# One recurrence chunk's values by quarters, output products by kind, bonus steps and one projection tile moved

## The reference

```python
def step(S, inp):
    r_t, w_t, k_t, v_t, kk_t, a_t = inp
    s_kk = jnp.einsum('bhij,bhj->bhi', S, kk_t)
    S = (S * w_t[:, :, None, :]
         - s_kk[..., None] * (a_t * kk_t)[:, :, None, :]
         + v_t[..., None] * k_t[:, :, None, :])
    return S, jnp.einsum('bhij,bhj->bhi', S, r_t)
...
wkv = (wkv7_scan(r4, heads(decay(w0_f, wf_lo, w_up_f)), k_f, v4, kk, heads(a_f), False)
       + wkv7_scan(r4, heads(decay(w0_b, wb_lo, w_up_b)), k_b, v4, kk, heads(a_b), True))
...
bonus = ((jnp.sum(r4 * k_f * rk, axis=-1, keepdims=True)
          + jnp.sum(r4 * k_b * rk, axis=-1, keepdims=True)) * v4).reshape(B, T, RWKV_DIM)
```

## Time and profile before

| | |
|---|---|
| median of 3 timed runs | 1910.21 us |
| lowest, highest | 1906.68, 1910.99 us |
| profiled execution, its own time | 1912.8 us |
| its span, first to last instruction | 1911.0 us |
| mean granted clock of PE | 0.95 of full speed |
| PE busy | 1721.5 us, 90% |
| PE weight loads busy | 1374.7 us, 72% |
| DVE busy | 921.0 us, 48% |
| ACT busy | 304.5 us, 16% |
| POOL busy | 171.5 us, 9% |

### The profile page before, as it was taken

How to read it: one execution, slowest core, us unless ns; L and a number is a source line. 1 busy time by engine, 2 the same in 40 slices (tenths; PEclk the granted TensorE clock), 3 DMA queues, 4 the chain that set the end, 5 groups by cost and what they waited for, 6 DMA issues and landing times.

```text
span 1911.0 us, 30563 instructions
## 1 busy us (share of the span) xinstructions
PE 1721.5 (90%) x12568; PEld 1374.7 (72%) x12568; DVE 921.0 (48%) x1848; ACT 304.5 (16%) x691; POOL 171.5 (9%) x159
## 2 busy tenths in 40 slices
PE   8999999999999999999999999999999765655666
PEld 3888888999888989679999998887787221211213
DVE  5766667897886366644676136852532000000000
ACT  2200000011210002422111114322323000000001
POOL 3000000000133310001000003630001000000000
PEclk9999999999999999999999999998999887888878
DMA  9433443765852214126545863102378999999996
GB/s 376 143 131 129 132 132 125 260 222 179 323 203 92 85 48 152 66 86 224 197 162 179 296 206 129 66 25 89 110 300 354 432 429 435 430 429 435 431 429 292
DMA packets 47336, 428.23 MB, mean 224 GB/s; under 512 B 5395, under 2 KB 6004, under 8 KB 16124
## 3 DMA queue, kind: packets, MB, share of 16 engines
q1 hardware_dynamic: 37584, 389.07, 52.8%
q10 hardware_dynamic: 9644, 37.59, 5.8%
HBM read 425.59 MB, written 1.05 MB: 223 GB/s over the span
## 4 chain that ended last, share of the span: by engine, by line
PE 70%; DMA 18%; DVE 7%; issue 2%; ACT 2%; POOL 0%; POOLq 0%; SPq 0%; ACTq 0%; DVEq 0%
DMA arena<-experts_ring_dram 18%; PE bank L1081 17%; PE bank L1215 14%; PE bank L1265 9%; PE bank L1311 6%; PE bank L1722 3%; PE bank L1411 3%; PE bank L1409 3%; PE bank L1793 2%; PE bank L2104 2%; PE bank L1589 1%; ACT arena L2408 1%; DVE tiny L3336 1%; PE bank L1464 1%; PE bank L1454 1%
## 5 line engine op out<-in xcount | busy, mean ns | idle before, releaser
L1081 PE MATMUL bank<-arena 128*128 128x128 f32 (+1 forms) x2208 | 355.7, 323 | 0.5 <-ACT arena L2629 0.5
L1081 PEld LDWEIGHTS bank<-arena 128*128 128x128 f32 x2208 | 325.5, 192 | 28.4 <-issue 1.8
L2104 PE MATMUL bank<-arena 128*32 128x512 f32 x1400 | 218.5, 780 | 140.2 <-DMA arena<-experts_ring_dram 140.2
L2104 PEld LDWEIGHTS bank<-arena 128*32 128x32 f32 x1400 | 58.8, 138 | 293.2 <-issue 293.1
L1215 PE MATMUL bank<-arena 128*128 128x256 f32 x880 | 193.9, 379 | 0.0
L1215 PEld LDWEIGHTS bank<-arena 128*128 128x128 f32 x880 | 167.1, 190 | 23.1 <-issue 0.5
L1265 PE MATMUL bank<-arena 128*128 128x128 f32 x1456 | 162.9, 275 | 0.0
L1265 PEld LDWEIGHTS bank<-arena 128*128 128x128 f32 x1456 | 162.8, 192 | 0.1
L3745 DVE TENSOR_TENSOR arena<-arena,bank 128x512 f32<-128x512 f32 x8 | 5.5, 688 | 238.2 <-PE bank L2104 238.2
L1311 PE MATMUL bank<-arena 128*128 128x128 f32 x880 | 102.8, 275 | 0.0
L1311 PEld LDWEIGHTS bank<-arena 128*128 128x128 f32 x880 | 100.9, 192 | 0.2
(11 more groups left out here) (533 smaller groups left out, 2480.9 us busy)
## 6 DMA issues: line engine op xcount, KB each, us to landing
arena<-dense_dram SPq DMA_DIRECT2D x169, 1024.0 KB, 4.9
arena<-experts_ring_dram SPq DMA_DIRECT2D x41, 4096.0 KB, 26.9
arena<-ada_rest_dram ACTq DMA_DIRECT2D x56, 512.0 KB, 4.6
arena<-experts_dram SPq DMA_DIRECT2D x18, 1024.0 KB, 9.4
arena<-ada_head_dram SPq DMA_DIRECT2D x8, 1024.0 KB, 23.9
arena<-experts_dram SPq DMA_DIRECT2D x10, 512.0 KB, 9.1
arena<-tokens_dram ACTq DMA_DIRECT2D x1, 2048.0 KB, 21.0
arena<-experts_ring_dram SPq DMA_DIRECT2D x1, 2048.0 KB, 23.9
```

The costliest lines, as they stand in the source:

```text
L1081: ins = mm(out, lhsT=w, rhs=rhs(k), start=k == 0, stop=k == k_tiles - 1)
L2104: ins = mm(ps[banks[half]][32 * e:32 * e + 32, :], lhsT=lhs[:, 2 * kp + par, CAP * e:CAP * e + CAP], rhs=slab[e][par][:, half * 512:half * ...
```

## The change

On PE, the sixth `aq` tile goes ahead of `own_products(0)` and of the wait for `keys_ready` 1, and ACT copies it ahead of the own blocks. On POOL, the five bonus steps behind the addition go behind the first chunk's last `level_part`. The second chunk's wanted values are made in column halves: 128x64 weights for the first kind, all of them first, and 64x64 quarters for the kind against the state, so 32 + 32 products where there were 16 + 16; PE takes all four banks ahead of them. The tails' products are grouped by kind: the state's for both directions first (second chunk alone), then for each direction the values' for all heads, a wait for U, and U's for all heads. A bank's start flag is given only with its first products.

```diff
@@ -1016,12 +1016,7 @@
             pool.wait_ge(kd_ready, 2)
             nc.gpsimd.tensor_tensor(rkk, kd256[:, 0:4, :], kd256[:, 4:8, :], add).then_inc(rk_step, 1)
             nc.gpsimd.memset(page(19, 2048), 0.0).then_inc(am_zero, 1)
-            pool.wait_ge(rk_step, 1)
-            for j in range(4):
-                nc.gpsimd.tensor_scalar(rkk[:, j, :], rkk[:, j, :], c("rk", j), None, mult).then_inc(rk_step, 1)
             nc.gpsimd.memset(page(20, 2048), 0.0).then_inc(am_zero, 1)
-            pool.wait_ge(rk_step, 5)
-            nc.gpsimd.tensor_tensor(rkk, rkk, US[:, US_R:US_R + 4, :], mult).then_inc(rk_step, 1)
@@ -1050,6 +1045,12 @@
                     if s == 0 and lv == 1:
                         pool.wait_ge(keys_ready, 3)
                         nc.gpsimd.memset(page(21, 2048), 0.0).then_inc(am_zero, 1)
+                if s == 0:
+                    pool.wait_ge(rk_step, 1)
+                    for j in range(4):
+                        nc.gpsimd.tensor_scalar(rkk[:, j, :], rkk[:, j, :], c("rk", j), None, mult).then_inc(rk_step, 1)
+                    pool.wait_ge(rk_step, 5)
+                    nc.gpsimd.tensor_tensor(rkk, rkk, US[:, US_R:US_R + 4, :], mult).then_inc(rk_step, 1)
@@ -1696,8 +1697,6 @@
-            pe.wait_ge(keys_ready, 1)
-            own_products(0)
             bl = [st.block() for _ in range(KD)]
             take(pe, "aq", AQ_BANKS[5], 0)
...
             ins.then_inc(full[AQ_BANKS[5]], 1)
+            pe.wait_ge(keys_ready, 1)
+            own_products(0)
             pe.wait_ge(keys_ready, 2)
             keys_to_tokens(0)
             keys_to_tokens(1)
@@ -1770,17 +1771,21 @@
                 for d in range(2):
                     for b in WV_BANKS[1][d]:
                         take(pe, "wv1", b, 0)
+                for j in range(4):
+                    for par in range(2):
+                        for d in range(2):
+                            for o64 in (lo64, hi64):
+                                hd = 2 * j + par
+                                mm(ps[WV_BANKS[1][d][par]][o64, 64 * j:64 * j + 64], lhsT=AM[:, 8 * d + hd, o64],
+                                   rhs=Vtok[:, 1 - d, 64 * hd:64 * hd + 64], start=j == 0, stop=False)
+                for d in range(2):
                     for j in range(4):
-                        for par in range(2):
-                            hd = 2 * j + par
-                            mm(ps[WV_BANKS[1][d][par]][:, 64 * j:64 * j + 64], lhsT=AM[:, 8 * d + hd, AM_KQ:AM_KQ + P],
-                               rhs=Vtok[:, 1 - d, 64 * hd:64 * hd + 64], start=True, stop=False)
                         row = 8 * d + 2 * j + 1 - d
-                        for par, r64 in enumerate((lo64, hi64)):
-                            b = WV_BANKS[1][d][par]
-                            ins = mm(ps[b][:, 64 * j:64 * j + 64], lhsT=QQ[r64, 2 * row, :], rhs=state_v[r64, d, j, :],
-                                     start=False, stop=True)
-                            if j == 3:
+                        for par, q_ in ((0, 0), (1, 1), (0, 1), (1, 0)):
+                            b, r64, o64 = WV_BANKS[1][d][par], (lo64, hi64)[par], (lo64, hi64)[q_]
+                            ins = mm(ps[b][o64, 64 * j:64 * j + 64], lhsT=QQ[r64, 2 * row, o64], rhs=state_v[r64, d, j, :],
+                                     start=False, stop=j == 3)
+                            if j == 3 and q_ != par:
                                 ins.then_inc(full[b], 1)
@@ -1863,21 +1868,25 @@
+                if s:
+                    for d in range(2):
+                        take(pe, "tail1", 5 * d, 0)
+                        for j in range(4):
+                            for par, r64 in enumerate((lo64, hi64)):
+                                mm(ps[5 * d][r64, j * P:j * P + P], lhsT=state_v[r64, d, j, :],
+                                   rhs=QQ[r64, 2 * (8 * d + 2 * j + 1 - d) + 1, :], start=j == 0, stop=False)
                 for d in range(2):
                     ch = d if s == 0 else 1 - d
+                    if s == 0:
+                        take(pe, "tail0", 5 * d, 0)
+                    for hd in range(HEADS):
+                        o = ps[5 * d][64 * (hd % 2):64 * (hd % 2) + 64, hd // 2 * P:hd // 2 * P + P]
+                        mm(o, lhsT=Vtok[:, ch, 64 * hd:64 * hd + 64], rhs=AM[:, 8 * d + hd, AM_KR:AM_KR + P],
+                           start=s == 0 and hd < 2, stop=False)
                     evacuated(pe, f"tail{s}", U_BANKS[d], 0)
-                    take(pe, f"tail{s}", 5 * d, 0)
-                    for j in range(4):
-                        row = 8 * d + 2 * j + ch
-                        heads = [(2 * j + par, ps[5 * d][64 * par:64 * par + 64, j * P:j * P + P]) for par in range(2)]
-                        for hd, o in heads:
-                            mm(o, lhsT=Vtok[:, ch, 64 * hd:64 * hd + 64], rhs=AM[:, 8 * d + hd, AM_KR:AM_KR + P],
-                               start=True, stop=False)
-                        for hd, o in heads:
-                            ins = mm(o, lhsT=nU[d][:, hd, :], rhs=AM[:, 8 * d + hd, AM_BR:AM_BR + P], start=False, stop=s == 0)
-                        if s:
-                            for r64, (hd, o) in zip((lo64, hi64), heads):
-                                ins = mm(o, lhsT=state_v[r64, d, j, :], rhs=QQ[r64, 2 * row + 1, :], start=False, stop=True)
+                    for hd in range(HEADS):
+                        o = ps[5 * d][64 * (hd % 2):64 * (hd % 2) + 64, hd // 2 * P:hd // 2 * P + P]
+                        ins = mm(o, lhsT=nU[d][:, hd, :], rhs=AM[:, 8 * d + hd, AM_BR:AM_BR + P], start=False, stop=hd >= HEADS - 2)
                     ins.then_inc(full[5 * d], 1)
@@ -2548,10 +2557,10 @@
             for k in range(3):
                 if k == 1:
-                    own_blocks(0)
                     b = AQ_BANKS[5]
                     got(act, "aq", b, 0)
                     A(va, ps[b][:, 0:T].rearrange("p (k n) -> p k n", n=P), ACT.Copy).then_inc(evac[b], 1)
+                    own_blocks(0)
```

## The result

| | before | changed |
|---|---|---|
| median of the timed runs, us | 1909.15 (4 runs) | 1897.63 (4 runs) |
| lowest to highest, us | 1906.68 to 1910.99 | 1896.58 to 1898.38 |
| span of the profiled execution, us | 1911.0 | 1896.2 |

The ratio is 0.994, with a 95% interval of 0.9923 to 0.9957: 11.5 us faster, beyond the 0.2% that a measurement can tell. Forecast: 1896.9 us, range 1893 to 1903, with a gain of 13.3 us. The forecast started from a median before of 1910.21 us; a fourth run has brought that to 1909.15, which is 1.1 of the 1.8 us between the gains.

A forecast was written before the change was run, and what follows sets the result against it. PE's work before 1400 us was taken to bound the kernel by setting the start of the expert-weight stream. Terms 2.6 + 6.1 + 2.4 + 2.2 = 13.3 us, from a median of 1910.2 to 1896.9 us; range 1893 to 1903.

The forecast's parts named there:

- The start: Ahead of the first level: bonus steps moved behind the levels and band tile moved first save 2.6 us, bounds 1.2 to 3.5.
- The step on line 1024: POOL's last bonus step held DVE's line 3515 at 3.25 us; with it moved, keys are ready 2.0 us earlier.
- the tile is behind PE and not ahead of it: At the start: PE does the 3.9 us band tile before the keys, so the next transposes start at 1212.7, not 1216.
- The values: Second chunk's values: narrower products take 3.4 us plus 0.5 waiting instead of 9.99, 6.1 us less; lower bound 4.0.
- The clock behind: Behind the second chunk's values: far and gate products at clock 1.00 instead of 0.50, 2.4 us less; 0 at the other end.
- The tails: Second chunk's tail takes 5.4 us for 7.6, 2.2 us less, bounds 0.3 to 2.8; first chunk's tail unchanged.
- A: Rival: the clock falls in the second chunk all the same; gain 8.4 us, 1901.8 us; chance 0.14.
- B: Rival: the values' column halves don't overlap, 75 ns a record; gain 10.7 us, 1899.5 us; chance 0.08.
- C: Rival: the gain doesn't reach the end, the expert stream hanging on something other than PE; 1910 us; chance 0.06.
- D: Rival: slower, the levels themselves fall to half clock; 16.7 us slower, 1926.9 us; chance 0.04.

The follow-up runs named there:

- e2_tile: Only the last band tile and its copy moved ahead of the own products, in the kernel before; 1909.54 us, ratio 0.9997.
- e4_tail: Only the tails' products grouped by kind, in the kernel before; 1907.06 us, ratio 0.9984.
- e3_quarters: Only the second chunk's values made as in the change, in the kernel before; 1900.89 us, ratio 0.995.
- e8_banks: Changed kernel with the values' first kind made direction by direction, the second direction's banks taken only then; 1895.33 us, ratio 0.993.
- e10_as_changed: The changed kernel run again without any further edit; 1896.76 us, ratio 0.9935.
- e5_one_half: Changed kernel with the values' first kind ordered as all 32 records of one column half, then all 32 of the other; 1896.43 us, one run.
- e7_wide: Changed kernel with the values' first kind again in 128x128 weights, the second kind left in quarters; 1898.25 us, taken once.
- e12_by_kind: Changed kernel with the second chunk's values grouped by kind but in the old wide weights for both kinds; 1899.70 us, one run.
- e11_mixed: Changed kernel with both kinds of the second chunk's values in quarters, but alternating for each pair of heads; 1897.48 us, one run.
- e6_last_step: Kernel before with only the last bonus step (line 1024) moved behind the levels, the four multiplications left in place; 1907.97 us, once.

## Why the prediction was right

**The start**, 2.6 us forecast, 3.15 measured, with a wrong split. The step on line 1024 held: without it DVE's product takes one undisturbed run. What failed is "What is gained is that the tile is behind PE and not ahead of it". Alone, the tile's move gains nothing, because POOL's masks wait for DVE's late products whatever PE does (6.28 us behind the value transposes in e2_tile, 6.27 in e4_tail); beside the bonus move it costs 0.2 to 0.4 us (15.11 to 15.14 in the seven profiles with it, 14.73 and 14.89 in the two without), because it delays the own products and so the masks. With the keys early, PE has the same work ahead of the first level in either order, and I had costed only one of them. So the term came out near its size for a reason that it did not have. About 1 us of the gain is clock and not a steady one: e3_quarters and e4_tail, which leave the start as it was, waited 2.84 and 2.82 us for the keys and kept 1.00 in the own products (64 records in 1.16 us), with 17.26 and 17.24 us to the second pair products instead of 18.28. Against these two the gain is 2.1 us. One sign of being wrong that the prediction named did come, in small: the first level waits for POOL, 0.17 us.

**The values**, 6.1 forecast, 6.39 measured. The products came at 3.01 us for 3.4, the wait at 0.52 for 0.5. The pace of the halves was read from the right row (34 ns there, 31 here), and the quarters went at 16 ns for 19. The reason was half of the truth: I put the whole term on the narrower weights, while the table gives 2.0 us of it to grouping and 2.35 to the clock, which had fallen within the old products. The price of 150 ns for a wide record held a share of a switch; it is 115 when wide records follow each other.

**The clock behind**, 2.4 forecast, 1.66 measured. The level was right; why the new orders keep it is not shown. Most of the difference is a break inside the far products: 1.63 to 1.64 us from their start to the gate products, in both profiles of the changed kernel at the same record, while six other kernels take 1.03 to 1.08 (e3_quarters 1.37). With it gone (e8_banks, 1292.29 to 1297.84) the stretch is 5.55 us, 2.24 less than before. What makes the break is open: the trace only says "issue", and it goes with small changes of the program ahead of it.

**The tails**, 2.2 forecast, 2.09 measured: 5.54 us for 5.4. The 32 records against the state take 59 ns each (1307.51 to 1309.41) and not 49. The gain itself is 14 switches of row height fewer (16 before, 2 after), at 0.15 us each.

**The end.** The terms measured are 3.15 + 6.39 + 1.66 + 2.09 = 13.3 us, the same sum as forecast. That it agrees so closely is luck: the start and the values gave 0.84 us more than their terms and the other two 0.85 less, and about 1 us of the start is the clock. 0.5 is lost again because the transposes began that much later in this execution, and 12.84 us reached the expert stream. The two profiled spans differ by 14.8 and the medians by 11.5. In the chain, the last piece begins 13.15 us earlier (1875.34 before, 1862.19 after) and takes 30.94 us before and 29.27 here; in e10_as_changed, the same kernel, it took 30.84. So 1.7 us of the 14.8 is scatter at the very end. The range was added up loosely: the bounds as stated give 14.8 us at the upper end (no upper one is given for the values, and 15.5 needs 0.7 more than their 6.1), and 10.0 and not 9.5 with the low ends of A and B left out. Rivals A, B, C and D did not happen. For B, e5_one_half shows what it would have looked like: 57 ns a record with one half after the other, 31 as the change has it. The Trainium skill's rule ("TensorE: Matmul & The Clock Gate", Part 3) that weights load beside a product only where row groups differ isn't what these runs show for column halves: both orders use all rows, so by the rule their pace would be the same, and it is 57 against 31 ns. Against A stand nine profiles at 1.00 with any of the new orders.

## What to carry to other kernels

Group small products by their row height and, within a group, make them in column halves that alternate: each was worth 2 to 2.6 us of 7.6 here, and they add. Before moving work into an engine's wait, ask what else hangs on the same late signal; here a tile of 3.7 us covered the wait for the keys and gained nothing, and only removing the wait's cause helped. An operation of POOL on SBUF that is running when DVE's critical product is issued can hold that product until it ends (here 2.0 us of POOL's 3.38), so a step whose result is wanted late belongs behind the levels.

## What the runs showed of the hardware

The granted clock fell to 0.50 while PE was busy 5.00 of 5.00 us, in each of the five profiles with wide, alternating products, and in none of the nine with another order or width. What in them the clock looks at was not settled: width alone (e7_wide), width with grouping (e12_by_kind) and alternation alone (e11_mixed) all kept 1.00, in one profile each.

A switch between products of 128 and of 64 rows costs some 0.15 us: alternating values have 15 of them and grouped ones one, and these 14 lie between 5.15 and 3.01 us, and again between 7.64 and 5.62. The second tail agrees: 14 switches fewer and 2.09 us less (7.63 to 5.54).

Two operations of the same form on DVE took 3.25 and 1.21 us; the longer one ran beside POOL's line 1024, and with that operation moved (e6_last_step) it took 1.23. POOL's four multiplications took 7.65 us beside DVE's products and 3.62 in their new place.
